# Token projections in chunk pairs with seven products, and their moves on GpSimd

## The chip, the core and the metric

The kernel runs on one core of one Trainium2 chip. The metric is the device time of one execution in microseconds. Before the change it is 1633.08 us, the median of 3 runs (1633.03 to 1633.43). The profile is of one further execution.

## The reference

One encoder block over 256 tokens of 2048 channels, in fp32. A combined projection of the normalised tokens feeds three parallel branches (gated short convolution, differential attention, cross-attention into 256 memory tokens); they are gated, merged and projected, and a gated feed-forward layer with a short convolution follows. The weights are read once: w_in is 2048 x 7168, w_mem_kv 2048 x 2048, w_gate 2048 x 6144, w_up 2048 x 11264, w_down 5632 x 2048. Abridged:

```python
def rmsnorm(x, g):
    xf = x.astype(jnp.float32)
    y = xf * lax.rsqrt(jnp.mean(xf * xf, axis=-1, keepdims=True) + EPS)
    return (y * g.astype(jnp.float32)).astype(x.dtype)
...
        h = rmsnorm(x, g_mix_pre[l])
        proj = h @ w_in[l]
        cb, cc, cv, dq, dk, dv, xq = jnp.split(proj, IN_OFFSETS, axis=-1)
        y_conv = short_conv_mixer(cb, cc, cv, conv_w[l]) @ w_conv_out[l]
        y_diff = diff_attention(...) @ w_diff_out[l]
        y_cross = memory_cross_attention(xq, rmsnorm(mem, g_mem[l]), w_mem_kv[l]) @ w_cross_out[l]
        gates = jax.nn.sigmoid(h @ w_gate[l] + b_gate[l])
        g_a, g_b, g_c = jnp.split(gates, N_BRANCH, axis=-1)
        x = x + rmsnorm((g_a * y_conv + g_b * y_diff + g_c * y_cross) @ w_o[l], g_mix_post[l])
        h = rmsnorm(x, g_ffn_pre[l])
        gate, val = jnp.split(causal_dwconv(h @ w_up[l], ffn_conv_w[l]), 2, axis=-1)
        x = x + rmsnorm((jax.nn.silu(gate) * val) @ w_down[l], g_ffn_post[l])
```

## The kernel before

Weights stream from HBM in blocks of 256 rows (KB = 2 K tiles of 128) by 512 columns (CW), 512 KB each, into a ring of 4 slots `raw`. Each product of fp32 matrices is made of three float32r matmuls. ScalarE rounds a block to `w_hi` (a copy, 128x1024 elements), VectorE forms `w_lo` = raw - w_hi, both in rings of 4 as well, and TensorE multiplies: for each of the 2 K tiles and each of the 2 token tiles (128 tokens), a_hi x w_hi, a_hi x w_lo and a_lo x w_hi, 12 matmuls of 128x512 in all. Such a block is a unit. The transposed tokens lie in SBUF as `hT_hi` and `hT_lo` (16 K tiles x 256 tokens), those of the memory as `memT_hi` and `memT_lo`.

The stages follow each other: projections (18 chunks `proj` of 512 columns with 8 units each; chunks 0 and 1 are mv, 2 and 3 mk, 4 and 5 xq, 6 cc, 7 cv, 8 cc, 9 cv, 10 and 11 cb, 12 and 13 dq, 14 and 15 dk, 16 and 17 dv), three branches with their gates, the output projection, up, down. Chunks 0 to 3 multiply the memory, 4 to 17 the tokens. A chunk accumulates in two PSUM banks of `ACC[c % 2]`, one bank for each token tile.

The queues are written by hand, engine by engine, and each engine runs its own in order. Semaphores count units: `hi_ready`, `lo_ready`, and `block_done` for units that TensorE has ended. ScalarE writes w_hi of unit n only when `block_done` says n-3, that is, when unit n-4 has ended; TensorE waits for `lo_ready`. SyncE loads block n when w_lo of block n-4 is made.

Between the units the queues of ScalarE, VectorE and TensorE hold the chunk steps (the loops over `proj` from L758, L1207 and L1777). A chunk that must be transposed is evacuated by ScalarE into `proj_stage` (step 3 of the next chunk; a cv chunk by VectorE, `evacuate_conv`), then 16 DMAs move squares of 32 tokens between partitions into `proj_moved` (`move_squares_proj`, SyncE, during the chunk after next), and VectorE transposes 32x32 blocks (`turn_squares`, step 2 of that chunk). For cv chunks ScalarE's `first_tap` (step 3) and VectorE's `turned_conv` (step 4) make the convolution; for cb chunks VectorE makes `y_tmp` (step 2) and `y_conv_lo` (step 4). The cross-attention of head h lies in the chunks from 7 + h on (CROSS_STEP): scores on TensorE in step 0, maximum on VectorE in step 3, exponent on ScalarE in step 4, normalising on VectorE in step 5; then 16 DMAs (`move_cross`, half on ScalarE's queue, half on SyncE's); the transposes of `p_crossT` on VectorE in step 4 of the next chunk, the product with the values on TensorE in its step 5, y_cross_hi and y_cross_lo in step 1 of the one after.

The normalised tokens reach `hT` by the same way: ScalarE's copies, 16 DMAs a quarter issued by GpSimd (`move_x`, L618), VectorE's transposes. After that GpSimd has nothing until the heads of the differential attention. The down stage already multiplies some of its blocks in groups of 11 units (`seven`) with seven products in place of eight: four differences of weight blocks on VectorE (`difference`), token sums (`left_sums`), and a `fold` at the end.

## Time and profile before

| | |
|---|---|
| median of 3 runs | 1633.08 us |
| the profiled execution's own time | 1633.22 us |
| its span, first to last instruction | 1631.4 us |
| TensorE, matmuls | 1621.4 us busy, 7225 |
| VectorE | 1090.4 us busy, 1463 instructions |
| ScalarE | 859.0 us busy, 1080 |
| GpSimd | 54.4 us busy, 117 |
| DMA | 346.75 MB, 213 GB/s in the mean |

The profile names TensorE PE, VectorE DVE, ScalarE ACT, GpSimd POOL; a q behind a name is its DMA issue queue, PEld are weight loads. Times in a timeline are in us from the start of the span. Matmuls are pipelined, so each row's duration overlaps the next; the distance of their starts is what counts. The projections end at about 420 us, the down stage runs from about 1393 us.

### The profile page before, as it was taken

Reading aid. Unit: us, or ns where it says so; the run is one execution under the profiler, and the core shown is the slowest. Engines: PE = TensorE matmul, PEld = TensorE weight load, DVE = VectorE, ACT = ScalarE, POOL = GpSimd, SP = SyncE. Lnnn points to the kernel's source line nnn. Section 1 sums busy time; section 2 is a strip of 40 time slices with the busy share of each in tenths; the row PEclk is TensorE's granted clock in tenths of the full one; section 3 lists DMA queues with packets and bytes.
Section 4 is the critical chain, followed back from the end, with each engine's and each line's share of the span. In section 5 each row is a group of like instructions: output and inputs, shape, how many; then the busy total and the mean of one; then the engine's idle time right before and its main releaser. Section 6 shows DMA issues by size and latency. Waiting matters only on the chain.

```text
span 1631.4 us, 21990 instructions
## 1 busy us (share of the span) xinstructions
PE 1621.4 (99%) x7225; PEld 1337.7 (82%) x7225; DVE 1090.4 (67%) x1463; ACT 859.0 (53%) x1080; POOL 54.4 (3%) x117
## 2 busy tenths in 40 slices
PE   9999999999999999999999999999999999999998
PEld 7888888888888888888888888888888888888886
DVE  5654565655566666666665757777667677799886
ACT  6744444444444444444445656656665665555553
POOL 2500000000000000000000000000000000000000
PEclk9999999999999999999999999999999999999999
DMA  8877666777666766676666477777777777666564
GB/s 283 284 218 217 196 185 188 228 214 217 191 206 196 236 208 211 193 234 211 222 223 225 125 221 216 219 219 220 217 219 215 211 216 224 217 221 204 193 207 155
DMA packets 207788, 346.75 MB, mean 213 GB/s; under 512 B 28953, under 2 KB 52330, under 8 KB 207210
## 3 DMA queue, kind: packets, MB, share of 16 engines
q1 hardware_dynamic: 201033, 342.48, 67.3%
q0 software_dynamic: 2048, 2.10, 0.4%
q10 hardware_dynamic: 4640, 1.33, 0.3%
q8 instruction: 37, 0.61, 0.2%
q14 instruction: 30, 0.24, 0.0%
HBM read 318.02 MB, written 2.10 MB: 196 GB/s over the span
## 4 chain that ended last, share of the span: by engine, by line
PE 96%; DVE 1%; DMA 1%; SPq 0%; ACT 0%; issue 0%; POOL 0%; DVEq 0%; ACTq 0%; POOLq 0%
PE PS L1724 24%; PE PS L1725 24%; PE PS L1726 24%; PE PS L1856 3%; PE PS L1858 3%; PE PS L1857 3%; PE PS L1971 3%; PE PS L1973 3%; PE PS L1972 3%; PE PS L1956 1%; PE PS L1958 1%; PE PS L1957 1%; PE PS L1894 1%; PE PS L1892 1%; PE PS L1893 1%; DMA raw<-in_w_down_dram 1%
## 5 line engine op out<-in xcount | busy, mean ns | idle before, releaser
L1112 DVE TENSOR_TENSOR w_lo<-raw,w_hi 128x1024 fp32r<-128x1024 f32 x479 | 582.8, 1223 | 454.0 <-ACT w_hi L676 452.8
L676 ACT ACTIVATE w_hi<-raw 128x1024 fp32r<-128x1024 f32 x479 | 504.9, 1059 | 497.6 <-PE PS L1726 436.3
L1724 PE MATMUL PS<-w_hi,hT_hi 128*128 128x512 f32 x1504 | 587.7, 391 | 0.0
L1726 PE MATMUL PS<-w_hi,hT_lo 128*128 128x512 f32 x1504 | 585.2, 389 | 0.0
L1725 PE MATMUL PS<-w_lo,hT_hi 128*128 128x512 f32 x1504 | 585.2, 389 | 0.0
L1724 PEld LDWEIGHTS PS<-w_hi,hT_hi 128*128 128x128 f32 x1504 | 282.3, 188 | 61.4 <-issue 2.7
L1726 PEld LDWEIGHTS PS<-w_hi,hT_lo 128*128 128x128 f32 x1504 | 282.3, 188 | 58.8
L1725 PEld LDWEIGHTS PS<-w_lo,hT_hi 128*128 128x128 f32 x1504 | 282.3, 188 | 58.1
L1030 ACT ACTIVATE w_hi<-raw 128x1024 fp32r<-128x1024 f32 x81 | 85.6, 1059 | 67.9 <-PE PS L1973 40.8
L1586 DVE TENSOR_TENSOR w_lo<-raw,w_hi 128x1024 fp32r<-128x1024 f32 x81 | 97.8, 1219 | 23.6 <-ACT w_hi L1030 22.3
L1971 PE MATMUL PS<-w_hi,act_hi 128*128 128x512 f32 x240 | 93.5, 389 | 0.0
L1972 PE MATMUL PS<-w_lo,act_hi 128*128 128x512 f32 x240 | 93.4, 389 | 0.0
L1973 PE MATMUL PS<-w_hi,act_lo 128*128 128x512 f32 x240 | 93.4, 389 | 0.0
L1971 PEld LDWEIGHTS PS<-w_hi,act_hi 128*128 128x128 f32 x240 | 45.0, 188 | 9.6 <-issue 0.4
L1973 PEld LDWEIGHTS PS<-w_hi,act_lo 128*128 128x128 f32 x240 | 45.0, 188 | 9.4
L1972 PEld LDWEIGHTS PS<-w_lo,act_hi 128*128 128x128 f32 x240 | 45.0, 188 | 9.3
L1724 PE MATMUL PS<-w_hi,memT_hi 128*128 128x512 f32 x124 | 48.6, 392 | 0.4 <-DVE memT_lo L1120 0.4
L1726 PE MATMUL PS<-w_hi,memT_lo 128*128 128x512 f32 x124 | 48.3, 390 | 0.0
L1725 PE MATMUL PS<-w_lo,memT_hi 128*128 128x512 f32 x124 | 48.3, 389 | 0.0
L965 ACT ACTIVATE up_stage<-PS,r_h 128x512 f32<-128x512 f32 x44 | 27.9, 685 | 36.7 <-PE PS L1726 36.4
L1726 PE MATMUL PS<-w_hi,mixT_lo 128*128 128x512 f32 x96 | 37.3, 389 | 0.0
L1724 PE MATMUL PS<-w_hi,mixT_hi 128*128 128x512 f32 x96 | 37.3, 389 | 0.0
(243 smaller groups left out, 1634.2 us busy)
## 6 DMA issues: line engine op xcount, KB each, us to landing
raw<-in_w_up_dram SPq DMA_DIRECT2D x176, 512.0 KB, 4.0
raw<-in_w_in_dram SPq DMA_DIRECT2D x112, 512.0 KB, 4.1
raw<-in_w_gate_dram SPq DMA_DIRECT2D x96, 512.0 KB, 4.5
raw<-in_w_down_dram SPq DMA_DIRECT2D x88, 512.0 KB, 4.4
raw<-in_w_mem_kv_dram SPq DMA_DIRECT2D x32, 512.0 KB, 5.8
raw<-in_w_o_dram SPq DMA_DIRECT2D x32, 512.0 KB, 4.3
up_moved<-up_stage SPq DMA_DIRECT2D x352, 32.0 KB, 2.8
raw<-in_w_conv_out_dram SPq DMA_DIRECT2D x16, 512.0 KB, 3.7
```

The costliest lines, as they stand in the source:

```text
L676: nc.scalar.activation(w_hi[i % RING][:], raw[i % RING][:], ACT.Copy).then_inc(hi_ready, inc)
L1030: nc.scalar.activation(w_hi[n % RING][:], src[:], ACT.Copy).then_inc(hi_ready, 1)
L1112: nc.vector.tensor_tensor(w_lo[i % RING][:], raw[i % RING][:], w_hi[i % RING][:].bitcast(F32), ALU.subtract).then_inc(lo_ready, inc)
L1586: nc.vector.tensor_tensor(w_lo[n % RING][:], src[:], w_hi[n % RING][:].bitcast(F32), ALU.subtract).then_inc(lo_ready, 1)
L1724: nc.tensor.matmul(o, a_hi, b_hi, start=first, stop=False)
L1725: nc.tensor.matmul(o, a_hi, b_lo, start=False, stop=False)
L1726: last = nc.tensor.matmul(o, a_lo, b_hi, start=False, stop=last_k)
L1856: nc.tensor.matmul(ACC[1][:, t, :], hi[:, k, s], w_hi[i % RING][:, c, :], start=k == 0, stop=False)
L1857: nc.tensor.matmul(ACC[1][:, t, :], hi[:, k, s], w_lo[i % RING][:, c, :], start=False, stop=False)
L1971: nc.tensor.matmul(C_bank(cc, t), act_hi[:, k, s], b_hi, start=first and c == 0, stop=False, skip_group_check=not first)
L1972: nc.tensor.matmul(C_bank(cc, t), act_hi[:, k, s], b_lo, start=False, stop=False, skip_group_check=not first)
L1973: last = nc.tensor.matmul(C_bank(cc, t), act_lo[:, k, s], b_hi, start=False, stop=c == KB - 1, skip_group_check=not first)
```

## The change

Seven pairs of chunks, (4, 5) to (16, 17), no longer multiply their first four K tiles plainly. There the tokens (2 token tiles x 2 groups of two K tiles) and the weights (2 groups x 2 chunks) form 2 x 2 blocks, and these are multiplied as seven products instead of eight. A product (`proj_product`) is one token tile by one block: 6 matmuls. The sums of tokens, `T_hi` and `T_lo`, are made once, at the start of chunk 3 (`token_sums`: one addition of 128x1024, four of 128x256, then a w_hi-like and a w_lo-like split). For each pair VectorE makes four differences of weight blocks (128x1024) and two folds (one PSUM bank plus a copy `q5`), ScalarE two copies of a bank.

The group of a pair c (`proj_group`) has 11 units u to u+10: the seven products are u, u+2, u+4, u+5, u+7, u+8 and u+10, and between them stand units 4 to 7 of the odd chunk before, as u+1, u+3, u+6 and u+9. After it come units 2 to 7 of chunk c and units 2 and 3 of chunk c+1. The steps 2 to 7 of the odd chunk before are placed inside the group by the table `ODD` (`THIRD` in the first group). Three pairs of banks are in use: even chunks use banks 0 and 1, odd ones 2 and 3 or 4 and 5.

Two of a pair's blocks are loaded by SyncE into `side` buffers ahead (`side_load`), the others through the ring; the bytes are the same. The 16 moves of each chunk and of each head, 256 in all, are issued by GpSimd, in the order shown, and no longer by SyncE and ScalarE.

Left out of the diff below are the tables of units and slots, the loads, and the step functions of each engine, which hold the same steps as before.

```diff
+    PAIRS = range(4, NP, 2)
+    G_UNITS = 11
+    N_BR = NP * CB + 3 * len(PAIRS)
+    RING_LOADS = NP * CB - 2 * len(PAIRS)
...
+        ODD = {1: (2,), 3: (3,), 5: (4,), 7: (5,), 8: (6,), 9: (7,)}
+        THIRD = {1: (4,), 3: (5,), 6: (6,), 9: (7,)}
...
+        def p_passed(c, u):
+            if u == G_UNITS - 1:
+                return [(c, 0)]
+            return [(c - 1, i) for i in (THIRD if c == PAIRS[0] else ODD).get(u, ())]
...
+            def move_squares_proj(c):
+                k = TI[proj[c]]
+                pool.wait_ge(evacuated[c % 2], c // 2 + 1)
+                if k:
+                    pool.wait_ge(turned_done, k)
+                for a in range(P // SQ):
+                    for m in range(P // SQ):
+                        pool.dma_start(proj_moved[SQ * m:SQ * (m + 1), a, :, :].rearrange("p q n -> p (q n)"),
+                                       proj_stage[SQ * a:SQ * (a + 1), m, :, :, :].rearrange("p b t n -> p (b t n)")).then_inc(proj_in, 16)
+            def move_cross(h):
+                pool.wait_ge(x_norm, h + 1)
+                if h:
+                    pool.wait_ge(x_pT, h)
+                for a in range(P // SQ):
+                    for m in range(P // SQ):
+                        pool.dma_start(p_moved[SQ * m:SQ * (m + 1), a, :, :].rearrange("p q n -> p (q n)"),
+                                       p_stage[SQ * a:SQ * (a + 1), m, :, :].rearrange("p q n -> p (q n)")).then_inc(x_pT_in, 16)
+            for c in (2, 3, 4, 5):
+                move_squares_proj(c)
+            move_cross(0)
+            move_squares_proj(7)
+            move_cross(1)
+            move_cross(2)
+            move_squares_proj(9)
+            move_cross(3)
+            for c in range(10, 16):
+                move_squares_proj(c)
...
+                if i == (3 if c <= 3 else 4) and c and not (c > 3 and c % 2):
+                    after_projection(c - 1)
+                if c == 3 and i == 1:
+                    act.wait_ge(t_sums, 5)
+                    nc.scalar.activation(T_hi[:], T_sum[:], ACT.Copy).then_inc(t_hi_done, 1)
...
+            def proj_group(c):
+                u, g = p_group[c], PAIRS.index(c)
+                B12, B22, E, q5 = p_side(c)
+                def after(k):
+                    for b in p_passed(c, k):
+                        proj_step(*b)
+                proj_split(c, 0)
+                if g:
+                    after_projection(c - 2)
+                proj_split(c - 1, 4)
+                after(1)
+                proj_hi(u + 2, E, (p_sums, 4 * g + 1))
+                proj_split(c - 1, 5)
+                after(3)
+                act.wait_ge(block_done, u + 1)
+                nc.scalar.activation(p_bank(c)[:, 0, :], p_bank(c)[:, 1, :], ACT.Copy).then_inc(p_seed, 1)
+                proj_hi(u + 4, E, (p_sums, 4 * g + 3))
+                proj_split(c, 1)
+                after(5)
+                proj_split(c - 1, 6)
+                after(6)
+                act.wait_ge(block_done, u + 3)
+                if g:
+                    act.wait_ge(p_folds, 2 * g)
+                nc.scalar.activation(q5[:], p_bank(c + 1)[:, 1, :], ACT.Copy).then_inc(p_seed, 1)
+                proj_hi(u + 7, B12, (p_sums, 4 * g + 2))
+                after(7)
+                proj_hi(u + 8, B22, (side_in[1], 16 * (g + 1)))
+                after(8)
+                proj_split(c - 1, 7)
+                after(9)
+                proj_hi(u + 10, E, (p_sums, 4 * g + 4))
+                after(10)
...
+            def proj_group(c):
+                u, g = p_group[c], PAIRS.index(c)
+                B12, B22, E, q5 = p_side(c)
+                b11, b21 = (raw_p[p_at[c, i] % RING] for i in range(2))
+                def after(k):
+                    for b in p_passed(c, k):
+                        proj_step(*b)
+                def difference(dst, a, b):
+                    nc.vector.tensor_tensor(dst[:], a[:], b[:], ALU.subtract).then_inc(p_sums, 1)
+                proj_split(c, 0)
+                dve.wait_ge(side_in[0], 16 * (g + 1))
+                if g == 0:
+                    dve.wait_ge(prep_turned, NCH)
+                    dve.wait_ge(squares, 2)
+                elif g == 1:
+                    dve.wait_ge(block_done, p_end(3))
+                else:
+                    dve.wait_ge(lo_ready, p_group[c - 2] + G_UNITS)
+                difference(E, B12, b11)
+                proj_split(c - 1, 4)
+                after(1)
+                dve.wait_ge(side_in[1], 16 * (g + 1))
+                dve.wait_ge(p_sums, 4 * g + 1)
+                difference(B12, B22, B12)
+                proj_lo(u + 2, E)
+                dve.wait_ge(lo_ready, u + 3)
+                difference(E, B22, E)
+                proj_split(c - 1, 5)
+                after(3)
+                proj_lo(u + 4, E)
+                k = p_at[c, 1]
+                dve.wait_ge(raw_in_p[k % RING], 16 * (k // RING + 1))
+                dve.wait_ge(lo_ready, u + 5)
+                difference(E, b21, E)
+                proj_split(c, 1)
+                after(5)
+                proj_split(c - 1, 6)
+                after(6)
+                proj_lo(u + 7, B12)
+                after(7)
+                dve.wait_ge(block_done, u + 5)
+                dve.wait_ge(p_seed, 2 * g + 2)
+                nc.vector.tensor_tensor(p_bank(c + 1)[:, 0, :], p_bank(c)[:, 1, :], q5[:], ALU.add).then_inc(p_folds, 1)
+                proj_lo(u + 8, B22)
+                after(8)
+                proj_split(c - 1, 7)
+                after(9)
+                proj_lo(u + 10, E)
+                dve.wait_ge(block_done, u + 8)
+                nc.vector.tensor_tensor(p_bank(c + 1)[:, 1, :], p_bank(c)[:, 1, :], q5[:], ALU.add).then_inc(p_folds, 1)
+                after(10)
...
+            for c in PAIRS:
+                proj_group(c)
+                for i in range(2, CB):
+                    proj_split(c, i)
+                    if i == 2:
+                        proj_step(c, 1)
+                    proj_step(c, i)
+                proj_split(c + 1, 2)
+                proj_step(c + 1, 0)
+                proj_split(c + 1, 3)
+                proj_step(c + 1, 1)
...
+            def proj_product(u, o, hi, lo, start=False):
+                pe.wait_ge(lo_ready, u + 1)
+                for k in range(KB):
+                    b_hi, b_lo = hi_p[u % RING][:, k, :], lo_p[u % RING][:, k, :]
+                    nc.tensor.matmul(o, hi[:, k, :], b_hi, start=start and k == 0, stop=False, skip_group_check=not start)
+                    nc.tensor.matmul(o, hi[:, k, :], b_lo, start=False, stop=False, skip_group_check=not start)
+                    last = nc.tensor.matmul(o, lo[:, k, :], b_hi, start=False, stop=k == KB - 1, skip_group_check=not start)
+                last.then_inc(block_done, 1)
...
+            def proj_group(c):
+                u, g = p_group[c], PAIRS.index(c)
+                X, Y = p_bank(c)[:, 1, :], p_bank(c + 1)[:, 1, :]
+                def block(a, k, t):
+                    return a[:, KB * k:KB * (k + 1), t * P:(t + 1) * P]
+                def after(k):
+                    for b in p_passed(c, k):
+                        proj_step(*b)
+                pe.wait_ge(evacuated[0], c // 2)
+                pe.wait_ge(prep_lo, 2 * (NCH + 1))
+                proj_product(u, X, block(hT_hi, 0, 0), block(hT_lo, 0, 0), True)
+                proj_multiply(c - 1, 4)
+                after(1)
+                pe.wait_ge(evacuated[1], c // 2 - 1)
+                pe.wait_ge(t_ready, 1)
+                if g == 0:
+                    pe.wait_ge(lo_ready, u + 3)
+                    nc.tensor.matmul(p_bank(c + 1)[:, 0, :], T_hi[:, 0, 0, :], hi_p[(u + 2) % RING][:, 0, :], start=True, stop=True)
+                proj_product(u + 2, Y, T_hi[:, 0, :, :], T_lo[:, 0, :, :], True)
+                proj_multiply(c - 1, 5)
+                after(3)
+                pe.wait_ge(p_seed, 2 * g + 1)
+                proj_product(u + 4, X, T_hi[:, 1, :, :], T_lo[:, 1, :, :])
+                proj_product(u + 5, p_bank(c)[:, 0, :], block(hT_hi, 1, 0), block(hT_lo, 1, 0))
+                after(5)
+                proj_multiply(c - 1, 6)
+                after(6)
+                pe.wait_ge(p_folds, 2 * g + 1)
+                proj_product(u + 7, X, T_hi[:, 2, :, :], T_lo[:, 2, :, :])
+                after(7)
+                proj_product(u + 8, p_bank(c + 1)[:, 0, :], T_hi[:, 3, :, :], T_lo[:, 3, :, :])
+                after(8)
+                proj_multiply(c - 1, 7)
+                after(9)
+                pe.wait_ge(p_folds, 2 * g + 2)
+                proj_product(u + 10, X, block(hT_hi, 1, 1), block(hT_lo, 1, 1))
+                after(10)
```

## Rows read from the trace of the kernel before

**Rows 1.** The page's first part: busy us, share of the span, instructions.
```profile
PE 1621.4 (99%) x7225; PEld 1337.7 (82%) x7225; DVE 1090.4 (67%) x1463; ACT 859.0 (53%) x1080; POOL 54.4 (3%) x117
```
**Rows 2.** All waits of TensorE: us in total, times, longest.
```profile
PE PS L1745 <- POOL ident L596: 1.6, 1, 1.6
PE PS L1724 <- DVE memT_lo L1120: 0.4, 1, 0.4
PE PS L1739 <- ACT mem_plain L682: 0.3, 1, 0.3
```
**Rows 3.** Timeline of TensorE, projections: start, us, engine, line, op, tiles, shape.
```profile
190.15 1.89 PE L1805 MATMUL PS<-mkT,xqT 128*128 128x256 f32 x8
...
292.09 0.39 PE L1724 MATMUL PS<-w_hi,hT_hi 128*128 128x512 f32 x1
...
294.81 0.39 PE L1724 MATMUL PS<-w_hi,hT_hi 128*128 128x512 f32 x1
```
**Rows 4.** Timeline of ScalarE, projections.
```profile
264.37 1.25 ACT L730 ACTIVATE proj_stage<-PS,r_x 128x512 f32<-128x512 f32 x2
265.51 1.70 ACT L737 ACTIVATE convT<-proj_turned,vecs 128x256 f32<-128x256 f32 x4
267.11 1.05 ACT L676 ACTIVATE w_hi<-raw 128x1024 fp32r<-128x1024 f32 x1
...
292.35 1.06 ACT L676 ACTIVATE w_hi<-raw 128x1024 fp32r<-128x1024 f32 x1 [0.71 <-PE PS L1726]
```
**Rows 5.** Timeline of VectorE, projections.
```profile
43.71 1.23 DVE L1112 TENSOR_TENSOR w_lo<-raw,w_hi 128x1024 fp32r<-128x1024 f32 x1 [1.49 <-ACT w_hi L676]
...
219.26 1.66 DVE L1149 SCALAR_TENSOR_TENSOR convT<-proj_turned,vecs,convT 128x255 f32<-128x255 f32 x4
...
222.53 0.88 DVE L1269 STREAM_TRANSPOSE p_crossT<-p_moved 128x128 f32<-128x128 f32 x4
223.34 1.18 DVE L1112 TENSOR_TENSOR w_lo<-raw,w_hi 128x1024 fp32r<-128x1024 f32 x1
...
242.56 0.69 DVE L1247 TENSOR_REDUCE top<-PS 128x2 f32<-128x512 f32 x1
...
286.42 1.42 DVE L1188 STREAM_TRANSPOSE proj_turned<-proj_moved 128x256 f32<-128x256 f32 x4
287.88 1.23 DVE L1201 TENSOR_TENSOR y_tmp<-proj_turned,convT 128x1024 f32<-128x1024 f32 x1
...
293.45 1.22 DVE L1112 TENSOR_TENSOR w_lo<-raw,w_hi 128x1024 fp32r<-128x1024 f32 x1 [0.36 <-ACT w_hi L676]
```
**Rows 6.** Timeline of VectorE, a group of the down stage.
```profile
1453.73 1.22 DVE L1586 TENSOR_TENSOR w_lo<-B_sum,w_hi 128x1024 fp32r<-128x1024 f32 x1
1454.98 1.23 DVE L1592 TENSOR_TENSOR B_sum<-raw,B_sum 128x1024 f32<-128x1024 f32 x1
1456.12 1.22 DVE L1586 TENSOR_TENSOR w_lo<-w_sum,w_hi 128x1024 fp32r<-128x1024 f32 x1
```
**Rows 7.** 40 us of down: busy us of PE, PEld, DVE, ACT, POOL, clock, DMA share.
```profile
1470.00:1510.00 40.00, 40.00 (x178) 33.14 (x177) 37.91 (x42) 22.83 (x26) 0.00 (x0) 1.00 0.61 205
```
**Rows 8.** Timeline of all engines where TensorE waits briefly, down stage.
```profile
1430.47 1.22 DVE L1586 TENSOR_TENSOR w_lo<-w_sum,w_hi 128x1024 fp32r<-128x1024 f32 x1
...
1431.28 0.39 PE L1958 MATMUL PS<-w_hi,S_lo 128*128 128x512 f32 x1
...
1431.74 0.50 PE L1956 MATMUL PS<-w_hi,S_hi 128*128 128x512 f32 x1
```
**Rows 9.** GpSimd's timeline, and issue to landing of its 64 moves.
```profile
42.29 7.81 POOL L618 DMA_DIRECT2D x_moved<-x_stage  x16 [2.38 <-ACT x_stage L780]
...
DMA to landing us min/median/max: 1.7/3.8/6.1
```
**Rows 10.** Timeline of VectorE: token sums of the down stage.
```profile
1443.93 1.22 DVE L1569 TENSOR_TENSOR whole<-act_hi,act_lo 128x1024 f32<-128x1024 f32 x1
...
1446.66 2.35 DVE L1586 TENSOR_TENSOR w_lo<-raw,w_hi 128x1024 fp32r<-128x1024 f32 x2
```

More of the change, by code:

```diff
@@ L823, in merge_hi @@
+            for i in range(4, CB):
+                proj_split(NP - 1, i)
+                if i == 4:
+                    after_projection(NP - 2)
+                    proj_step(NP - 1, 2)
+                    proj_step(NP - 1, 3)
+                proj_step(NP - 1, i)
             def merge_hi(j, src):
@@ L1208, in _ @@
+            for c in range(3):
                 for i in range(CB):
                     if c or i >= PLAIN:
[L1210 to L1216 removed]
@@ L1808, in _ @@
-                    h = c - CROSS_STEP - 1
-                    if 0 <= h < CH and i == 5:
-                        pe.wait_ge(x_pT, h + 1)
-                        if h:
-                            pe.wait_ge(x_lo, h)
-                        for db in range(2):
-                            for kb in range(NT):
-                                v0 = h * CHD + db * P
-                                last = nc.tensor.matmul(PS[:, 7, db * TOK:(db + 1) * TOK], mv_tok[:, kb, v0:v0 + P],
-                                                        p_crossT[:, kb, :], start=kb == 0, stop=kb == NT - 1)
-                        last.then_inc(x_oT, 1)
+                        proj_multiply(c, i)
@@ L1820, in branch_step @@
+            for i in range(4, CB):
+                proj_multiply(NP - 1, i)
+                if i == 4:
+                    proj_step(NP - 1, 2)
+                    proj_step(NP - 1, 3)
+                proj_step(NP - 1, i)
             def branch_step(r, j, jp):
```

569 lines of the change are left out of this document (350 added, 219 removed).

## The prediction, made before the changed kernel was run

> **What bounds the kernel now.** I read the page first: TensorE is busy in 1621.4 us of a span of 1631.4 us [rows 1]. Then the waits of TensorE: 1.6, 0.4 and 0.3 us, all in the first microseconds, and nothing after that [rows 2]. So from about 12 us on the time is the number of matmuls times their pitch. The timeline of TensorE gives that pitch: a unit (one 512 KB block of weights, 12 matmuls of 128x512) starts at 292.09, the next at 294.81, so 2.72 us for a unit and 0.2267 us for a matmul [rows 3]. A matmul taken away is worth 0.2267 us as long as nobody makes TensorE wait. What must be found is whether VectorE and ScalarE, which split each block into w_hi and w_lo, still keep ahead.
>
> **How far ahead they can be.** ScalarE writes w_hi of unit n once TensorE has ended unit n-4: with a unit starting at 292.09 the activation starts at 292.35, 0.26 later [rows 3, 4]. It takes 1.06, VectorE starts 0.04 later and takes 1.22 to 1.23 [rows 4, 5], and TensorE starts 0.05 after w_lo is written [rows 8]. The lead is thus three units less 2.64 us, and neither engine can save up more.
>
> **What is taken away.** A product has 6 matmuls, 1.36 us. Each of the seven pairs runs 7 products for 8: 42 matmuls, 9.52 us. One matmul is added (the first group's extra one), 0.23. Gross gain 9.29 us. Edits with one answer: the new order of slots and banks costs nothing; the 256 moves taken from SyncE and ScalarE free queues that TensorE did not wait for [rows 2], so they bring nothing.
>
> **What is added, by pair.** VectorE: 3 more w_lo, 4 differences, 2 folds. In the down stage such operations follow each other at 1.14 us, and at 1.25 where one needs the result of the one before [rows 6]. So 7 x 1.14 + 2 x 0.69 (a PSUM operation of that size, [rows 5]) = 9.4 us. ScalarE: 3 w_hi and 2 PSUM copies, about 4.3 us. All of it lies in the group of 11 units, which is 7 x 1.36 + 4 x 2.72 = 20.4 us on TensorE, while VectorE's 15 operations and folds take 18.5 to 19. This can be hidden: the same pattern in the down stage keeps VectorE busy for 37.91 of 40 us and TensorE for 40.00 [rows 7]. But in the projections the chunk steps (turning, convolution, cross-attention) sit between the units, and six of them (2 to 7 of the odd chunk) now fall inside the group. So each group is worked through. Time 0 is where TensorE starts unit u, the group's first. It would start u+1 at 1.36, u+2 at 4.08, u+3 at 5.44, u+4 at 8.16, u+5 at 9.52, u+6 at 10.88, u+7 at 13.60.
>
> Group of chunk 12. ScalarE may evacuate chunk 10 from -5.44 + 0.26 = -5.18; two activations, 1.14 [rows 4]; w_hi of u+1 is done at -2.99, VectorE's w_lo of it starts at -2.95. Then VectorE, by starts: turning of chunk 9 at -1.81 (1.42, [rows 5]), the second difference at -0.39, w_lo(u+2) 0.75, third difference 2.00 (it waits for the one before), w_lo(u+3) 3.14. ScalarE meanwhile: w_hi(u+3) from 0.26, the first convolution tap 1.22 to 2.82 (1.60, [rows 4]), the PSUM seed to 3.39, w_hi(u+4) to 4.43. So w_lo(u+4) starts at 4.47, fourth difference 5.72, w_lo(u+5) 6.86, and at 8.00 VectorE reaches step 4 of chunk 11: eight convolution operations, 219.26 to 222.53 = 3.27, and four transposes of the attention weights, to 223.34 = 0.81 [rows 5]. Only at 12.08 does it start w_lo(u+6), which TensorE gets at 12.08 + 1.28 = 13.36. TensorE was ready at 10.88: a wait of 2.48 us. Behind it, w_lo(u+7) and the fold end before TensorE needs them, so it is not repeated.
>
> The seed, a copy from PSUM to PSUM on ScalarE, is not in the trace. I take it like an evacuation of that size, 0.57 [rows 4]; at nothing w_hi(u+4) would follow the third difference and the wait be 2.4, at twice that 3.05.
>
> Group of chunk 10: the same taps and transposes; its scores (eight small matmuls, [rows 3]) give VectorE an earlier start and it has one reduction more (0.69, [rows 5]), but w_hi(u+4) again ends at 4.43 on ScalarE, and from there all is equal: 2.48 us.
>
> Group of chunk 14: the turn with the result awaited takes 1.46 [rows 5], y_tmp a pitch of 1.14 [rows 6], w_lo(u+3) comes at 5.60 for 5.44 (0.16), then y_conv_lo makes w_lo(u+6) come at 11.49 for about 11.15 (0.34): 0.5 us in two waits.
>
> Groups of 6 and 16 have a turn alone: w_lo(u+3) at 4.42 for 5.44, u+6 at 9.2 for 10.88, no wait. Group of 8 adds a reduction and a normalisation, which fit the 2.4 us that the later units have to spare. Before the first group chunk 3 carries the token sums: 1443.93 to 1446.66 for the same sums in the down stage, 2.73 us [rows 10], a split of 1.14, and x's last two turns and preparations; I find unit (4,0) ready 2.6 us before its turn and no wait.
>
> A wait costs more than itself: the first matmul after one takes 0.50 for 0.39 and starts 0.46 behind its predecessor [rows 8]. I take 0.15 for each of four waits. The trace has no wait of 2 us in mid-stream; the bounds for this are 0 and, if the clock fell for as long as the wait lasted, about 2 us each.
>
> Moves on GpSimd. Sixteen take 7.81 us to issue and 1.7 to 6.1 us to land, 3.8 in the median [rows 9]. An even chunk's move may start when the odd one before it is turned (-0.39), lands by 11.1 to 13.3, and is wanted by VectorE at about 17. An odd chunk's starts near -20.6 and lands by -7, wanted at -1.8. Cross move 0 starts near 11.8 in its group and lands by 23 to 26; VectorE wants it at 23.7 and the unit behind is not due before 30.3. The sums hold with some 3 to 8 us to spare, cost zero. Nothing waits behind these on GpSimd until the heads of the diff attention.
>
> GpSimd's 16 issues from 42.29 took 0.49 us each [rows 9], the w_lo of 43.71, with two operands in SBUF, 1.23 as ever [rows 5]. The Trainium skill (SBUF — State Buffer, Who interferes with whom) says that a VectorE instruction with two SBUF inputs blocks only what GpSimd reads, but that one in a 2-port mode keeps it from writing DMA descriptors; by the first half the moves cost nothing, by the second the normalisations of the cross-attention could stretch them. The row agrees with the first half, and none here shows the second.
>
> **Sum.** 9.29 - (2 x 2.48 + 0.50 + 4 x 0.15 = 6.06) = 3.2 us gained. The profiled execution took 1633.22 us, 0.14 above the median of the runs, 1633.08. 1633.22 - 3.2 = 1630.0 us. A measurement of this kernel tells about 0.2%, 3.3 us, from no change, so the forecast lies at that border (1629.8).
>
> **Rivals.**
> (a) VectorE keeps ahead after all, or the waits are much shorter, for instance because steps overlap more than their starts in the old trace show. Against it: at step 4 of chunk 9 and 11 it has 4.08 us of work to put in and 1.6 us to spare. For it: the down stage, where nothing waits. Time: 1633.22 - 9.3 = 1623.9, with half the waits 1627.
> (b) The moves come late: this ends slower. If GpSimd's issue stretches under a denser VectorE, cross move 0 decides first: VectorE has unit (8,5) ready at 11.8 + 15p + 3.5 + 0.81 + 1.28 for p us an issue, TensorE wants it at 30.3, so from p = 0.86 on. At p = 1.0 that is 2.1 us, as much for cross move 2, some 3 for chunk 7, whose move stands behind it in the queue, and the same again for chunk 9: about 10 lost, 1640. Measured p is 0.49, which speaks against it.
> (c) The waits of 2.5 us make the granted clock fall to its lower level (1.2 of 2.4 GHz) for a while. The stretch of the down stage shows 1.00 throughout [rows 7], but hardly a wait. If it fell for a time like the wait's, each would cost some 1 to 2 us: 1632 to 1634. The Trainium skill (TensorE: Matmul & The Clock Gate, What's actually happening) says that idleness throttles the clock; by that the two waits are where it would show.
> (d) The steps cost VectorE more than worked out, as in the second wait of each group: 1631 to 1634.
>
> **Chances.** Forecast with (d) 0.64, (a) 0.17, (b) 0.12, (c) 0.07. The forecast's own spread, 1628 to 1633, puts a little under half of its chance below 1629.8; with (a) that is 0.45 for faster. (c), the rest of the forecast: 0.43. Slower is (b): 0.12. For 8 in 10 the range goes from near (a), 1624.5, to 1635.5, which leaves out (b).
>
> **What would show it.** TensorE waits for w_lo of about 2.5 us in the groups of 10 and 12 before unit u+6, small ones in 14, none in 4, 6, 8 and 16; VectorE in the taps and p_crossT transposes meanwhile; 41 matmuls fewer of 128x512; x_moved-like issues at 0.49 us; waits of VectorE for DMA absent. Wrong if TensorE waits for p_crossT, for a fold or for a turned chunk, or if the waits sum to under 3 or over 9 us.

## The result, and the profile after

The changed kernel takes 1636.63 us (median of 20 runs, 1634.56 to 1639.67); the kernel before takes 1633.47 beside it (20 runs, 1632.88 to 1634.85). The ratio is 1.002, with a 95% interval of 1.0014 to 1.0027: 3.2 us slower where 3.2 us faster was forecast, and outside the range. The profiled execution took 1638.19 us, 1.6 above the median of its kernel, against 1633.22 of the one before.

The page of the changed kernel, its span and first part, to be read against [rows 1]:

```profile
span 1636.4 us, 22106 instructions
PE 1617.4 (99%) x7184; PEld 1332.9 (81%) x7184; DVE 1155.7 (71%) x1532; ACT 887.4 (54%) x1116; POOL 178.8 (11%) x373
```

The 41 matmuls are gone, but TensorE's busy time fell by 4.0 us and not by 9.3, and the span grew by 5.0. The waits of TensorE (us in total, times, longest), against [rows 2]:

```profile
PE PS L2064 <- DVE w_lo L1378: 6.0, 4, 3.1
PE PS L2022 <- POOL ident L670: 1.6, 1, 1.6
PE PS L2335 <- DVE w_lo L1863: 1.2, 1, 1.2
```

L2064 and L1378 are the matmul and w_lo of the projections, L2335 and L1863 those of the down stage. The first long wait, in the timeline of TensorE (start, us, engine, line, operation):

```profile
232.34 0.39 PE L2076 MATMUL PS<-w_hi,hT_lo 128*128 128x512 f32 x1
235.03 0.50 PE L2064 MATMUL PS<-w_hi,hT_hi 128*128 128x512 f32 x1 [2.30 <-DVE w_lo L1378]
235.37 0.39 PE L2065 MATMUL PS<-w_lo,hT_hi 128*128 128x512 f32 x1
...
236.63 0.63 PE L2064 MATMUL PS<-w_hi,hT_hi 128*128 128x512 f32 x1
237.05 0.63 PE L2065 MATMUL PS<-w_lo,hT_hi 128*128 128x512 f32 x1
237.48 0.63 PE L2066 MATMUL PS<-w_hi,hT_lo 128*128 128x512 f32 x1
```

The step from 232.34 to 235.03 (start to start) is 2.46 us longer than the pitch of [rows 3]. It is the wait ahead of unit u+6 of chunk 10's group. Then comes something else: from 236.63 on, the matmuls stand 0.42 to 0.43 us apart. The windows of the same places give the reason (us, busy time of PE, PEld, DVE, ACT and POOL, granted clock, DMA share, GB/s):

```profile
235.00:236.00 1.00, 0.97 (x4) 0.84 (x5) 1.00 (x1) 0.00 (x0) 0.00 (x0) 1.00 0.00 0
237.00:239.00 2.00, 2.00 (x6) 1.56 (x5) 2.00 (x4) 0.00 (x0) 1.14 (x3) 0.50 0.58 220
240.00:242.00 2.00, 2.00 (x11) 1.71 (x10) 1.42 (x2) 1.44 (x2) 2.00 (x5) 1.00 0.37 76
287.00:288.00 1.00, 0.00 (x0) 0.00 (x0) 1.00 (x2) 0.00 (x0) 0.00 (x0) 0.80 0.00 0
288.00:290.00 2.00, 1.93 (x5) 1.55 (x6) 2.00 (x4) 0.00 (x0) 0.00 (x0) 0.50 0.39 59
```

After the wait TensorE worked at the full clock for 1.4 us, and then the granted clock was 0.50 (1.2 of 2.4 GHz) from 236.4 to 239.8: 3.4 us in which it does 1.7 us of work. In chunk 12's group the clock is low for 3.4 us as well, from 287.6 to 291.0. There it fell while TensorE still waited: the wait ended at 288.07, half a microsecond later. Added up over the starts, the matmuls of the two stretches lost 1.6 and 1.4 us. A slow matmul counts as busy, so this loss shows as busy time and not as a wait. It is 3.0 of the 5.3 us of busy time that 41 fewer matmuls did not give back. Another 1.0 lies in the first 15.6 us, where TensorE is busy 14.0 us for 13.0 before, and the rest in the first two matmuls behind each wait.

VectorE's timeline ahead of u+6, with the operations of [rows 5]:

```profile
228.57 1.22 DVE L1378 TENSOR_TENSOR w_lo<-raw,w_hi 128x1024 fp32r<-128x1024 f32 x1
229.71 1.66 DVE L1317 SCALAR_TENSOR_TENSOR convT<-proj_turned,vecs,convT 128x255 f32<-128x255 f32 x4
231.40 1.66 DVE L1322 SCALAR_TENSOR_TENSOR convT<-proj_turned,vecs,convT 128x254 f32<-128x254 f32 x4
232.98 0.89 DVE L1464 STREAM_TRANSPOSE p_crossT<-p_moved 128x128 f32<-128x128 f32 x4
233.79 1.18 DVE L1378 TENSOR_TENSOR w_lo<-raw,w_hi 128x1024 fp32r<-128x1024 f32 x1
```

Between the w_lo of u+5 and that of u+6 lie 4.08 us of step 4, as the working had it. In chunk 12's group the wait was longer, from 284.56 to 288.07, 3.3 us over the pitch, and one of 0.50 us preceded it at 278.48. Where the extra comes from begins 35 us ahead of that wait, in four rows, each from the timeline of its engine:

```profile
249.95 0.69 DVE L1442 TENSOR_REDUCE top<-PS 128x2 f32<-128x512 f32 x1 [3.43 <-PE PS L2094]
251.89 2.15 DVE L1338 SCALAR_TENSOR_TENSOR proj_stage<-PS,r_x,cc_sb 128x128 f32<-128x128 f32 x8
256.68 7.81 POOL L708 DMA_DIRECT2D proj_moved<-proj_stage  x16 [11.00 <-issue]
269.71 1.27 ACT L836 ACTIVATE proj_stage<-PS,r_x 128x512 f32<-128x512 f32 x2 [3.29 <-DMA proj_moved<-proj_stage]
```

VectorE waits 3.4 us for the scores, which TensorE now computes at the end of the group. So it evacuates chunk 9 late, until 254.0. GpSimd issues that chunk's moves only from 256.7, and ScalarE, which must write chunk 10 over the tile they read, waits 3.3 us for the last to land. Its w_hi are late by as much.

The last part of the loss is at the very end. SyncE's timeline, the output's eight stores:

```profile
1623.67 7.54 SPq L658 DMA_DIRECT2D out_dram<-y_down  x8
```

The last is issued at 1631.2, and the span ends 5.2 us later. In the kernel before the same row ends at 1628.9 and the span 2.6 us later. What grew is GpSimd's closing DRAIN, an instruction that the program ends with. It is not among the busy rows; the view of the line that ends the program shows it (ns shortest, middle, longest, then its start in us), first before, then after:

```profile
L80 POOLq DRAIN  x1: 5290/5290/5290, 1625.9 to 1625.9; - x1
L83 POOLq DRAIN  x1: 7903/7903/7903, 1628.3 to 1628.3; - x1
```

It starts 0.2 us after GpSimd's last operation (r_out) in both, and took 5.29 us before and 7.90 us after.

### The profile page after: what moved, and what is told of

Read it like the earlier page. It is cut to its first block, busy times and chain, and to the rows that moved or that the text cites. A ratio compares the mean times of both kernels' runs of the same rounds, so it can differ in the third digit from the quotient of the medians.

```text
span 1636.4 us, 22106 instructions
## 1 busy us (share of the span) xinstructions
PE 1617.4 (99%) x7184; PEld 1332.9 (81%) x7184; DVE 1155.7 (71%) x1532; ACT 887.4 (54%) x1116; POOL 178.8 (11%) x373
## 4 chain that ended last, share of the span: by engine, by line
PE 93%; DVE 4%; issue 1%; DMA 1%; ACT 1%; POOL 1%; DVEq 0%; SPq 0%; ACTq 0%; POOLq 0%
PE PS L2001 16%; PE PS L2002 16%; PE PS L2003 16%; PE PS L2064 6%; PE PS L2066 6%; PE PS L2065 6%; PE PS L2335 3%; PE PS L2336 3%; PE PS L2337 3%; PE PS L2220 3%; PE PS L2222 3%; PE PS L2221 3%; PE PS L2320 1%; PE PS L2321 1%; PE PS L2322 1%; PE PS L2074 1%
## 5 line engine op out<-in xcount | busy, mean ns | idle before, releaser
L1280 DVE TENSOR_TENSOR w_lo<-raw,w_hi 128x1024 fp32r<-128x1024 f32 x336 | 408.5, 1222 | 294.6 <-ACT w_hi L782 293.6
L782 ACT ACTIVATE w_hi<-raw 128x1024 fp32r<-128x1024 f32 x336 | 353.9, 1058 | 311.9 <-PE PS L2003 260.7
L2001 PE MATMUL PS<-w_hi,hT_hi 128*128 128x512 f32 x1056 | 411.8, 390 | 0.0
L2003 PE MATMUL PS<-w_hi,hT_lo 128*128 128x512 f32 x1056 | 410.9, 389 | 0.0
L2002 PE MATMUL PS<-w_lo,hT_hi 128*128 128x512 f32 x1056 | 410.8, 389 | 0.0
L2001 PEld LDWEIGHTS PS<-w_hi,hT_hi 128*128 128x128 f32 x1056 | 198.2, 188 | 43.5 <-issue 2.7
L2003 PEld LDWEIGHTS PS<-w_hi,hT_lo 128*128 128x128 f32 x1056 | 198.2, 188 | 41.5
L2002 PEld LDWEIGHTS PS<-w_lo,hT_hi 128*128 128x128 f32 x1056 | 198.2, 188 | 40.8
L1378 DVE TENSOR_TENSOR w_lo<-raw,w_hi 128x1024 fp32r<-128x1024 f32 x129 | 156.1, 1218 | 81.3 <-ACT w_hi L864 80.9
L864 ACT ACTIVATE w_hi<-raw 128x1024 fp32r<-128x1024 f32 x129 | 135.9, 1059 | 101.0 <-PE PS L2066 72.7
L2064 PE MATMUL PS<-w_hi,hT_hi 128*128 128x512 f32 x336 | 133.6, 398 | 6.0 <-DVE w_lo L1378 6.0
L2066 PE MATMUL PS<-w_hi,hT_lo 128*128 128x512 f32 x336 | 131.9, 392 | 0.0
L2065 PE MATMUL PS<-w_lo,hT_hi 128*128 128x512 f32 x336 | 131.7, 392 | 0.0
L1198 ACT ACTIVATE w_hi<-raw 128x1024 fp32r<-128x1024 f32 x81 | 85.6, 1059 | 68.8 <-PE PS L2337 40.8
L1863 DVE TENSOR_TENSOR w_lo<-raw,w_hi 128x1024 fp32r<-128x1024 f32 x81 | 97.8, 1220 | 25.3 <-ACT w_hi L1198 24.3
L708 POOL DMA_DIRECT2D proj_moved<-proj_stage x192 | 93.9, 498 | 141.9 <-ACT proj_stage L836 82.5
L2335 PE MATMUL PS<-w_hi,act_hi 128*128 128x512 f32 x240 | 93.4, 389 | 1.2 <-DVE w_lo L1863 1.2
L2064 PEld LDWEIGHTS PS<-w_hi,hT_hi 128*128 128x128 f32 x336 | 63.6, 189 | 21.2 <-DVE w_lo L1378 8.1
L2066 PEld LDWEIGHTS PS<-w_hi,hT_lo 128*128 128x128 f32 x336 | 63.6, 189 | 13.3
```

What stands on the lines that cost most here:

```text
L782: nc.scalar.activation(w_hi[i % RING][:], raw[i % RING][:], ACT.Copy).then_inc(hi_ready, inc)
L1280: nc.vector.tensor_tensor(w_lo[i % RING][:], raw[i % RING][:], w_hi[i % RING][:].bitcast(F32), ALU.subtract).then_inc(lo_ready, inc)
L1378: nc.vector.tensor_tensor(lo_p[u % RING][:], src[:], hi_p[u % RING][:].bitcast(F32), ALU.subtract).then_inc(lo_ready, 1)
L2001: nc.tensor.matmul(o, a_hi, b_hi, start=first, stop=False)
L2002: nc.tensor.matmul(o, a_hi, b_lo, start=False, stop=False)
L2003: last = nc.tensor.matmul(o, a_lo, b_hi, start=False, stop=last_k)
```

## Experiments

Theory 1: VectorE's convolution in step 4 makes the two long waits, they make the clock fall, and 256 more transfers by GpSimd lengthen the DRAIN. Theory 2: the moves or their queue hold up the projections.

**The moves alone.** The kernel before, with `move_squares_proj` and `move_cross` in GpSimd's program and gone from SyncE's and ScalarE's.

```diff
# SyncE
-                    if c >= 2 and proj[c - 2] in TI and i < P // SQ:
-                        move_squares_proj(c - 2, i)
-                    if 0 <= c - 1 - CROSS_STEP < CH and i in (4, 5):
-                        move_cross(c - 1 - CROSS_STEP, i - 2)
# ScalarE
-                            move_cross(h, 0)
...
-                            move_cross(h, 1)
# GpSimd
...
+            for c in (2, 3, 4, 5):
+                move_squares_proj(c)
+            move_cross(0)
...
```

> The kernel before with one part of the change alone: GpSimd issues all 256 moves of chunks and heads, in the order of the change; all products stay plain. Theory 1 (GpSimd's closing DRAIN grows with the DMAs that it has issued: 5.3 us with 64, 7.9 with 320): TensorE has no new wait, its last matmul ends as before, the DRAIN takes 7.9 us and the whole is 2.6 us slower than before, about +0.16%. Rival (the DRAIN waits for something else in the changed kernel, or its length is chance): DRAIN near 5.3 and the time of before within 0.05%. Second rival (late moves hold up VectorE already here): waits of TensorE for w_lo or p_crossT in the projections and more than 3 us lost.

Measured 1635.63 us (11 runs) against 1633.39 (27 runs), ratio 1.0014 (1.0005 to 1.0023). The projections are as before, with no wait of TensorE. The DRAIN takes 7.90 us and the span ends 5.2 us after the last store's issue. Waits of TensorE in the down stage:

```profile
PE PS L1975 <- DVE w_lo L1605: 0.9, 2, 0.7
PE PS L1990 <- DVE w_lo L1605: 0.3, 1, 0.3
```

So the moves cost some 2 us (2.2 by the medians), all far behind where they are, and nothing in the projections.

**The convolution later.** The changed kernel with one number changed.

```diff
-                if i == 4 and name == "cv":
+                if i == 7 and name == "cv":
                     turned_conv(...)
```

> The changed kernel with one step moved: VectorE's convolution operations of the cv chunks (3.27 us) stand at step 7 of chunks 9 and 11, that is behind unit u+9, instead of at step 4, ahead of u+6. Theory 1 (VectorE's steps make the two long waits, and these make the clock fall): both waits before u+6 shrink from 2.5 and 3.3 us to under 0.5, the two stretches of 3.4 us at the lower clock vanish, and the kernel gains 5.5 + 3 us less what remains, about 7: near 1629.5. Rival (late moves of GpSimd make the waits): the wait in the group of chunk 12 stays above 2 us, the clock still falls there, and the gain is about 4: near 1632.5.

Measured 1629.50 us (11 runs), ratio 0.9976 (0.9967 to 0.9985). Its waits of TensorE, and VectorE's timeline around u+6:

```profile
PE PS L2335 <- DVE w_lo L1863: 1.4, 1, 1.4
PE PS L2064 <- DVE w_lo L1378: 0.4, 2, 0.2
```
```profile
229.31 0.89 DVE L1464 STREAM_TRANSPOSE p_crossT<-p_moved 128x128 f32<-128x128 f32 x4
230.12 1.19 DVE L1378 TENSOR_TENSOR w_lo<-raw,w_hi 128x1024 fp32r<-128x1024 f32 x1
...
235.07 1.22 DVE L1378 TENSOR_TENSOR w_lo<-raw,w_hi 128x1024 fp32r<-128x1024 f32 x1
236.21 1.67 DVE L1317 SCALAR_TENSOR_TENSOR convT<-proj_turned,vecs,convT 128x255 f32<-128x255 f32 x4
```

Both long waits are gone and the clock falls nowhere in mid-stream. This one number is worth 7.1 us by the medians (1636.63 to 1629.50, with 1633.4 for the kernel before beside each). Between the two profiled executions it is 9.0 us, of which the two waits are 5.8 and the falls of the clock 3.0; the profiled execution of the changed kernel was slower than its median. Theory 1 holds for the steps.

**The waits filled.** The changed kernel, with matmuls in the two waits whose result nobody reads.

```diff
                 proj_product(u + 5, ...)
+                if c in (10, 12):
+                    pe.wait_ge(x_exp, 3 if c == 10 else 4)
+                    for _ in range(8 if c == 10 else 12):
+                        nc.tensor.matmul(PS[:, 6, :], hT_hi[:, 0, 0:P], T_hi[:, 0:2, :, :], start=True, stop=True)
```

> The changed kernel with matmuls of no use in the two long waits: 8 of 128x512 ahead of unit u+6 in the group of chunk 10, 12 in that of chunk 12, into a free PSUM bank (1.8 and 2.7 us of 2.5 and 3.3 us of waiting). They add nothing to the output. Theory 1 (the clock falls because TensorE stands idle in those waits): no stretch at the lower clock, units resume at the same moments, and the time is that of the changed kernel less the falls, 2 to 3.5 us less: 1633 to 1634.5. Rival (the clock falls for another reason, by its own rhythm or by the load after the wait): the falls stay and the time is that of the changed kernel, 1636.5.

Measured 1633.79 us (11 runs), ratio 1.0002 (0.9993 to 1.0011). The windows of both groups:

```profile
226.00:240.00 14.00, 13.51 (x60) 10.87 (x59) 13.82 (x26) 8.17 (x12) 2.39 (x5) 1.00 0.35 107
280.00:296.00 16.00, 15.58 (x70) 12.63 (x68) 15.65 (x27) 6.96 (x7) 0.99 (x3) 1.00 0.60 177
```

The weights of u+6 come no sooner, but the clock stays at 1.00, and 2.8 us come back. That is the price of the falls by themselves, measured with the waits' cause left in; the profile of the changed kernel has 3.0.

**The moves on SyncE.** The changed kernel with its moves issued by SyncE, eight at a time between its loads; GpSimd keeps its 64.

```diff
                 sp.dma_start(raw_p[k % RING][:], p_weights(c, i)).then_inc(raw_in_p[k % RING], 16)
+                for f, n, parts in AFTER.get((c, i), ()):
+                    f(n, parts)
...
```

> The changed kernel with the other part undone: the seven products stay, the 256 moves are issued by SyncE between its loads, GpSimd has only its 64 of before. Theory 1: GpSimd's DRAIN is back at 5.3 us, 2.6 us gained there; move 9 no longer lands late, so the wait in the group of chunk 12 falls from 3.3 to about 2.5; the convolution's waits and their clock falls stay. Together near 1633. Rival (moves on GpSimd cost nothing, all loss is in the groups): 1636.5, or more where SyncE's moves delay loads.

Measured 1667.40 us (5 runs), ratio 1.0211 (1.0197 to 1.0225): far off anything expected. Waits of TensorE, then of ScalarE:

```profile
PE PS L2082 <- DVE w_lo L1396: 15.9, 10, 3.5
PE PS L2092 <- DVE w_lo L1396: 12.6, 6, 8.6
```
```profile
ACT w_hi L882 <- DMA raw<-in_w_in_dram: 87.2, 24, 11.2
```

SyncE stands at a move until its chunk is evacuated, and the weight loads behind it start late: ScalarE waits for them, up to 11.2 us for one. It shows what moving them to GpSimd avoids at this placement, which was mine; it does not show that no placement on SyncE would do. The span ended 2.6 us after the last store's issue, as in the kernel before: with 64 transfers by GpSimd the tail is back, though the seven products are in.

This kernel also shows that the length of a wait does not decide by itself whether the clock falls. A wait of TensorE, and the windows around it and around a later one:

```profile
241.53 0.50 PE L2082 MATMUL PS<-w_hi,hT_hi 128*128 128x512 f32 x1 [2.94 <-DVE w_lo L1396]
```
```profile
102.00:256.00 154.00, 145.56 (x632) 117.41 (x630) 112.19 (x148) 80.99 (x102) 0.00 (x0) 1.00 0.59 192
298.50:300.70 2.20, 0.39 (x2) 0.00 (x0) 1.26 (x2) 1.85 (x2) 0.00 (x0) 1.00 0.10 23
301.50:304.80 3.30, 3.30 (x9) 2.55 (x8) 3.27 (x5) 0.54 (x1) 0.00 (x0) 0.50 0.97 318
```

The wait of 2.9 us that ended at 241.53 had no fall behind it, the clock stayed at 1.00 until 256. A wait of 1.8 us, from 298.9 to 300.7, was followed by one.

**The DRAIN earlier, and left out.** Both on top of the later convolution, and the first also on the kernel before.

```diff
# e7_drain_early, e9_before_drain_early: GpSimd, idle from some 930 us on
             for t in range(NT):
+                if t == 0:
+                    pool.drain()
                 pool.wait_ge(down_sum, t + 1)
# e8_no_drain
-        block = ctx.enter_context(nc.Block())
+        block = ctx.enter_context(nc.Block(no_gpsimd_drain=True))
```

> The changed kernel with the convolution at step 7 (as e2_conv_late), and with one DRAIN of GpSimd ahead of its wait for the first down sum, where it has been idle since about 936 us and stays so for some 680 us. In the kernel before the span ends 1.18 us after the last DMA packet (1630.26 to 1631.44), in all kernels with 320 GpSimd transfers 3.79 us after it. Theory (GpSimd's closing DRAIN works off the record of all its transfers, 5.29 us for 64, 7.90 us for 320, and an earlier DRAIN takes that work away from the end): the distance falls back to at most 1.18 us, so at least 2.6 us less than e2_conv_late: 1626.9 us, or a few tenths less. Rival (the closing DRAIN's length is fixed by what the queue was used for in the program, whoever drained before): 1629.5 us, distance 3.79 us.

> As e2_conv_late, but the program's block closes without GpSimd's DRAIN (the other engines drain, all meet at a barrier of semaphores; each GpSimd transfer has been waited for by its consumer long before). Theory: what lies between the last packet and the end of the span is 1.18 us or less, 1626.9 us or a few tenths less, the same as e7_drain_early. Rival (something else that grew with the GpSimd transfers, such as the queue's own teardown, makes the 2.6 us): 1629.5 us.

> The kernel before with the same early DRAIN of GpSimd. It has 64 GpSimd transfers, and its closing DRAIN of 5.29 us (1625.92 to 1631.21) ends 0.95 us after the last packet. Theory: if that DRAIN set the end, the kernel gains up to 1 us (1632.4 to 1633.4 us); if the landing of the last output set it, nothing (1633.4 us). Which of the two it is tells how much of the 2.6 us in the changed kernel was hidden: a gain here means that the closing DRAIN already cost in the kernel before. Rival (an early DRAIN itself costs, or delays the work behind it): slower than 1633.4 us by more than 0.3.

Measured: 1626.63 us (5 runs), ratio 0.9959 (0.9946 to 0.9972); 1626.83 us without the DRAIN (6 runs), the same ratio and interval; and 1633.18 us for the kernel before with it (11 runs), ratio 0.9999 (0.9991 to 1.0008), beside 1633.13 of before. Of the six executions without the DRAIN one took 5279.45 us; the other five took 1625.82 to 1626.94, and nothing on record tells whether the missing DRAIN had to do with it. The end of the first, with the early DRAIN and the closing one:

```profile
span 1624.9 us, 22106 instructions
```
```profile
1615.04 7.62 SPq L658 DMA_DIRECT2D out_dram<-y_down  x8
```
```profile
L763 POOLq DRAIN  x1: 7903/7903/7903, 925.1 to 925.1; - x1
L83 POOLq DRAIN  x1: 34/34/34, 1619.7 to 1619.7; - x1
```

The early DRAIN takes the 7.90 us, where GpSimd has nothing else to do, and the closing one 0.03. The last store is issued at 1622.7 and the span ends 2.2 us later, where it was 5.2 with the convolution at step 7 alone. Both ways of taking the DRAIN off the end bring 2.7 to 2.9 us (2.4 to 2.6 if each is taken against the kernel before beside it), so nothing else that grew with the moves stood there. In the kernel before its span ends 0.4 us sooner after the stores, too little to measure: there the DRAIN ended at 1631.2, 0.4 us after SyncE was done (1630.8), and it was almost only the growth that cost.

**How the DRAIN grows.** The kernel before with the four heads' moves by GpSimd (128 transfers of GpSimd in all), and with 32 and 160 small ones added while it is idle (96 and 224).

```diff
+                    for k in range(32):          # 160 in the other
+                        pool.dma_start(dose_sb[32 * (k % 4):32 * (k % 4 + 1), 0:8], ident[32 * (k % 4):32 * (k % 4 + 1), 0:8]).then_inc(dose_in, 16)
+                        if k % 4 == 3:
+                            pool.wait_ge(dose_in, 16 * (k + 1))
```

> The kernel before with only the four heads' moves (64 transfers) by GpSimd, so 128 GpSimd transfers in all. Theory (the closing DRAIN grows with their number, 2.61 us over 256 transfers): DRAIN 5.9 to 6.0 us, and the span ends 1.6 to 1.9 us after the last packet. Rival (it is a step, one length below some number and another above): 5.29 or 7.90 us.

> The kernel before with 32 more GpSimd transfers of 32 descriptors each (a few bytes of ident into a scratch tile), issued and waited for while GpSimd is idle between 936 and 1619 us: 96 in all. Measured so far: a closing DRAIN of 5.29 us after 64 transfers (0.083 us for each), from 1625.9 to about 1636.4 us, 10.5 us, after 128 (e10_cross_only, 0.082 each), 7.90 us after 320. Theory (each transfer still on record costs 0.082 us, and when 320 were issued all but 96 had been taken off the record on the way): 7.9 us, the span ends about 3.8 us after the last packet. Rival (the length hangs on what the transfers moved or on their semaphores, not on their number): 5.3 us, or anything else.

> The same with 160 more GpSimd transfers: 224 in all. Theory with one record that is cleared as a whole each time it is full at 224: 0.7 us or 18.4 us here; with a record that keeps only the youngest few: between 7.9 and 10.6 us. If the length is linear in the number with nothing taken off: 18.4 us, the span 14 us after the last packet. Rival as for e13_dose_96.

One execution each, beside 1632.8 to 1633.4 us of before: 1638.64 us with the heads' moves, 1636.18 with 96 transfers, 1633.97 with 224. The first is slower than the kernel with all 256 moves on GpSimd, with a quarter of them. The span on its page, its store row and its DRAIN, and the DRAIN with 224:

```profile
span 1636.6 us, 21988 instructions
```
```profile
1621.27 7.54 SPq L582 DMA_DIRECT2D out_dram<-y_down  x8
```
```profile
L80 POOLq DRAIN  x1: 10517/10517/10517, 1625.9 to 1625.9; - x1
L80 POOLq DRAIN  x1: 2677/2677/2677, 1627.0 to 1627.0; - x1
```

| transfers by GpSimd | last store's issue to end of span, us | DRAIN, us |
|---|---|---|
| 64 (before) | 2.6 | 5.29 |
| 96 | 5.2 | 7.90 |
| 128 | 7.8 | 10.52 |
| 224 | 2.2 | 2.68 |
| 320 (after) | 5.2 | 7.90 |

With 224 the DRAIN ended ahead of the landing of the last store, so it cost nothing. My expectation of a line through 64 and 320 was wrong, and so was each length that I had put down for 224. Up to 128 each transfer costs 0.082 us (5.29 / 64); then the DRAIN gets shorter. 320 take as long as 96, which is what I had said for 96. So part of the record is worked off on the way.

A place for it can be seen: ahead of its 193rd transfer GpSimd pauses. In all eight profiles with 320, that is the first move of chunk 9, 2.6 us after its data is ready (254.04 to 256.68 above); the first move of chunk 7, the 145th, follows its data after 0.3 us. In the kernel with 224 it is one of the added transfers, and it waits for nothing that the profile shows:

```profile
1106.30 1.96 POOL L660 DMA_DIRECT2D dose_sb<-ident  x4 [6.79 <-issue]
```

That is 6.8 us after the one before, where the added groups otherwise stand 1.3 to 4.6 us apart. What is left after 224, 2.68 us, is the price of 32 transfers (5.29 less 32 times 0.082 is 2.67), and 32 were issued from the 193rd on. That fits a record emptied at this pause. It doesn't explain 320, where 128 follow the pause and the DRAIN has the length of 96. By what rule the record is cleared is open.

**Chunk 9's evacuation sooner**, on top of the early DRAIN:

```diff
-                if i == 4 and c and proj[c - 1][0] == "cv":
+                if i == 2 and c and proj[c - 1][0] == "cv":
                     evacuate_conv(c - 1)
```

> e7_drain_early with the evacuation of a cv chunk by VectorE at step 2 of the group after it, instead of step 4, so that its moves by GpSimd start earlier. In the changed kernel ScalarE waited 3.29 us at 269.71 for the landing of that chunk's moves, and group 12 had 0.8 us more of waits than group 10. Theory (the moves' late start, set by VectorE's order, leaves the wait that is still there in group 12: 0.375 us at 293.48 and 0.107 us at 279.60 in e2_conv_late): 0.1 to 0.5 us less than e7_drain_early, no row of ScalarE's evacuation with an idle of 3 us before it. Rival (the evacuation at step 2 holds up w_lo of the group's first units, as the convolution did at step 4): waits of TensorE in groups 8, 12 or 16 grow by up to 1.3 us each, up to 3 us slower than e7_drain_early.

Measured 1625.22 us (5 runs), ratio 0.995 (0.9937 to 0.9963), 1.4 us less than with the early DRAIN alone. ScalarE's evacuation of chunk 10 without the edit, and then with it:

```profile
265.17 1.27 ACT L838 ACTIVATE proj_stage<-PS,r_x 128x512 f32<-128x512 f32 x2 [3.17 <-DMA proj_moved<-proj_stage]
```
```profile
264.33 1.27 ACT L838 ACTIVATE proj_stage<-PS,r_x 128x512 f32<-128x512 f32 x2 [1.66 <-PE PS L2068]
```

With it ScalarE waits for TensorE's bank again and not for a landing, and all waits of chunk 12's group are gone. They had been 0.39, 0.36 and three of 0.11 us at 274 to 295; I had counted two of them, hence the small miss. The down stage's wait was 0.5 us shorter in this profile, which is chance by the next run. This is the fastest version: 0.5% below the kernel before, 0.7% below the changed one.

**The changed kernel again.**

> The changed kernel once more, for what repeats. Theory: the two waits of TensorE of 2.5 us and 3.3 us over the pitch near 234 and 285 us, the 2.6 us between the end of the cv chunk's evacuation (254.05) and the first issue of its moves (256.68), and the wait of 1.2 to 1.3 us near 1410 us all come again within 0.1 us; the granted clock falls 0 to 3 times for 3.4 us each, and the span differs from 1636.4 us by about 1.7 us for each fall more or fewer. Rival (the 2.6 us or the wait near 1410 us are chance, a fetch of code or a stray packet): one or both are absent or of another size.

1639.39 us, span 1637.6. Its waits of TensorE:

```profile
PE PS L2064 <- DVE w_lo L1378: 6.2, 4, 3.1
PE PS L2335 <- DVE w_lo L1863: 1.6, 1, 1.6
```

The two long waits repeat (2.47 and 3.30 us over the pitch), so do the 2.6 us ahead of chunk 9's moves and two falls of the clock. The span is 1.2 us longer with the same number of falls, so these do not account for all that varies. The falls stand elsewhere against the waits: the first begins at 234.7, as TensorE resumes, the second at 289.3, 1.3 us after it has. The wait of the down stage does not keep its size: 1.3 us over the pitch in the first profile, 1.8 now, with 0.2 and 0.4 us lost a little later (0.2 in the first profile). It stands near 1401 to 1411 us in most kernels, from 0.1 us in the kernel before to 1.8; two versions of the kernel before have none there. In the changed kernel four of SyncE's issues there took 3.6 us for their usual 2.4, ahead of the load that was late. Why is open.

## Why the prediction was wrong

The mechanism of the forecast, VectorE's steps ahead of unit u+6, was right. Three steps of it failed: a wait's own price was put at 0.15 us and was the fall of the clock (3.0 us in the profile), the moves were put at zero and lengthened the DRAIN (2.6 us), and ScalarE's evacuation of chunk 10 was put too early (1.3 us). Term by term:

- **41 matmuls at 0.2267 us, 9.29 us**: right.
- **Group of chunk 10, 2.48 us**: measured 2.46, by the cause named. **Group of 14, 0.16 and 0.34**: measured 0.17 and 0.36, and two restarts of 0.11. **No wait in 4, 6, 8 and 16**: right.
- **Group of chunk 12, 2.48 us**: measured 3.79 in two waits. The step that failed is "ScalarE may evacuate chunk 10 from -5.18". It looked at the bank, and for the moves of an odd chunk only at when VectorE wants them (-1.8). ScalarE wants the same tile free 3.4 us earlier. The moves began at -16.6 instead of -20.6, behind VectorE's wait of 3.4 us for the scores and GpSimd's pause of 2.6.
- **A restart costs 0.15**: 0.11 where the clock stayed. At the two long waits the clock's fall was the price: 1.6 and 1.4 us, 3.0 in the profile, and 2.8 by the experiment that filled the waits. The mechanism was rival (c), with its size right (1 to 2 us each), but it had a chance of 0.07. I had held the lack of such a wait in the trace for a reason to take 0.15, when the bounds that I wrote down were 0 and 2. The Trainium skill (TensorE: Matmul & The Clock Gate, What's actually happening) says that idleness throttles the clock; the trace agrees, with 0.50 at both waits, though in the kernel with SyncE's moves a wait of 2.9 us had no fall behind it. The length of 3.4 us is the trace's, and so is the place: 1.4 us after TensorE had resumed at the first wait, 0.5 us before it did at the second.
- **"The moves cost zero", "nothing waits behind these on GpSimd until the heads"**: right for the projections. The issue stayed at 0.49 us (16 in 7.81) beside VectorE's w_lo, and rival (b) did not come. But behind the last instruction of GpSimd stood its DRAIN, which was in the trace of before, 5.29 us long and ending 0.2 us before the span did. I had worked through what the moves' consumers see and not what the engine does with 256 more of them: 2.6 us, at the one place where nothing hides it.
- **The down stage**: 1.2 us more lost to waits than before in the profile, of a kind that varies; the forecast had no term for it.

The sum for the profiled execution: forecast -3.2; +3.0 clock, +2.6 DRAIN, +1.3 chunk 12, +1.2 down stage. That is +4.9, and the span grew by 5.0; the other terms (chunks 10 and 14, the restarts, the first microseconds) are each off by 0.25 us or less. The median grew by 3.2 only. The changed kernel's executions differ in their mean granted clock, one fall of 3.4 us being 0.001 of it: spans of 1633.1 us in the mean at 0.998 (4 runs), 1634.6 at 0.997 (6), 1636.0 at 0.996 (7), 1636.9 at 0.995 (3). The profiled one is at 0.996. That the clock doesn't fall at every wait in every execution is only suggested by these means: two executions were profiled, with two falls each, and a mean moves without a fall too (0.997 to 0.998 in the kernel with the moves alone, whose profile has none in mid-stream).

Of the rivals, (a) and (b) did not come: no wait was shorter than worked out, no move was late for VectorE. (c) and, in chunk 12's group, (d) came on top of the forecast.

## What to carry to other kernels

When work is packed closer, put the long steps of the engine that feeds TensorE behind the group, not in it: a wait of 2.5 us cost 4.2 with the fall of the clock that followed it, and one number in the order was worth 7 us. Count for every added GpSimd transfer what it leaves for the DRAIN at the end of the program, and put a DRAIN where GpSimd is idle. Closing the block without it gained as much, but one of its six executions took 5279 us. For every tile that DMAs read, ask who wants to write it next, not only who reads their result.

## What the runs showed of the hardware

- The granted clock fell to 0.50 (1.2 of 2.4 GHz) for 3.4 us at waits of TensorE of 2.5 and 3.3 us, in two profiles of two. The fall began between 0.5 us before TensorE resumed and 1.4 us after. At the down stage's waits of 1.3 and 1.8 us it stayed at 1.00. Useless matmuls in the waits kept it at 1.00. In the kernel with SyncE's moves a wait of 2.9 us had no fall behind it and one of 1.8 us did, so these runs give no limit of length.
- GpSimd's closing DRAIN took 5.29 us after 64 transfers, 7.90 after 96, 10.52 after 128, 2.68 after 224, 7.90 after 320 and 0.03 behind an earlier DRAIN, although every transfer had landed hundreds of microseconds before.
- GpSimd starts its 193rd transfer 2.6 us after the data is ready, in eight profiles of eight.
